# Another order for the first loads, the output stored in four parts, and another PSUM bank for two first up products

## The reference

```python
def first_block(x, ...):
    for i in range(2):
        xn = rms_norm(x, norm_mix[i])
        y = moba_attention(xn, w_qkv, w_o, cos, sin) if i == 0 else pool_mixer(xn, pool_w, pool_scale)
        x = x + y
        h = relu(rms_norm(x, norm_mlp[i]) @ w_up)       # 1024 -> 4096
        x = x + (h * h) @ w_down                        # 4096 -> 1024
    return rms_norm(x, norm_final)
```

## Time and profile before

| what | value |
|---|---|
| median of 3 runs | 1211.26 us (1208.13 to 1212.42) |
| the profiled execution's own time | 1212.48 us |
| its span, first to last instruction | 1210.7 us |
| TensorE busy | 1154.4 us, 95% of the span |
| VectorE busy | 676.7 us, 56% |
| ScalarE busy | 530.9 us, 44% |
| mean granted TensorE clock | 0.984 |
| start of the first product | 19.28 us |

### The profile page before, as it was taken

One profiled execution on the slowest core, in us unless ns is written; L12 is line 12 of the kernel. 1 busy time (PEld: TensorE's weight loads), 2 busy tenths in 40 slices (PEclk: granted clock), 3 DMA queues, 4 the chain that ended last, 5 costly groups with the idle time before them and its releaser, 6 DMA issues.

```text
span 1210.7 us, 17821 instructions
## 1 busy us (share of the span) xinstructions
PE 1154.4 (95%) x7132; PEld 1019.1 (84%) x7132; DVE 676.7 (56%) x933; ACT 530.9 (44%) x640; POOL 43.5 (4%) x69
## 2 busy tenths in 40 slices
PE   4999899999999999997898999999999999999997
PEld 4887799999889999977677999999888668999996
DVE  4745554455665544566545655555845556554554
ACT  5446344344443443444444443345433455344342
POOL 0000000000000000000000000002300410000000
PEclk9999999999999999998899999999999899999999
DMA  9751445645535556455313565556653222556550
GB/s 350 250 186 56 154 158 189 207 169 178 191 99 195 170 190 205 145 136 191 105 35 104 174 195 180 180 191 209 207 191 136 62 91 66 178 174 200 181 173 35
DMA packets 127450, 196.37 MB, mean 162 GB/s; under 512 B 7392, under 2 KB 97632, under 8 KB 127280
## 3 DMA queue, kind: packets, MB, share of 16 engines
q1 hardware_dynamic: 124256, 186.29, 46.6%
q0 software_dynamic: 3152, 9.51, 2.6%
HBM read 194.73 MB, written 1.05 MB: 162 GB/s over the span
## 4 chain that ended last, share of the span: by engine, by line
PE 84%; DVE 10%; ACT 3%; issue 1%; DMA 1%; DVEq 0%; SPq 0%; ACTq 0%
PE ps L1306 26%; PE ps L1307 25%; PE ps L1308 25%; DVE wlo L854 2%; DVE xs L942 1%; ACT whi L596 1%; PE ps L1443 1%; PE ps L1705 1%; PE ps L1428 1%; ACT junk L609 1%; DMA raw<-attn_w_qkv_in 1%; DVE act_lo L956 1%; PE ps L1664 1%; PE ps L1328 1%; DVE x L987 1%
## 5 line engine op out<-in xcount | busy, mean ns | idle before, releaser
L854 DVE TENSOR_TENSOR wlo<-raw,whi 128x2048 fp32r<-128x2048 f32 (+2 forms) x176 | 395.9, 2266 | 182.1 <-ACT whi L596 181.7
L1306 PE MATMUL ps<-act_hi,whi 128*128 128x256 f32 x1384 | 392.6, 284 | 7.7 <-DVE act_lo L956 4.7
L1307 PE MATMUL ps<-act_lo,whi 128*128 128x256 f32 x1384 | 391.7, 283 | 0.0
L1308 PE MATMUL ps<-act_hi,wlo 128*128 128x256 f32 x1384 | 391.6, 283 | 0.0
L596 ACT ACTIVATE whi<-raw 128x2048 fp32r<-128x2048 f32 (+2 forms) x176 | 328.8, 1888 | 118.6 <-PE ps L1308 104.0
L1306 PEld LDWEIGHTS ps<-act_hi,whi 128*128 128x128 f32 x1384 | 263.6, 190 | 12.5 <-issue 9.6
L1307 PEld LDWEIGHTS ps<-act_lo,whi 128*128 128x128 f32 x1384 | 263.6, 190 | 2.0
L1308 PEld LDWEIGHTS ps<-act_hi,wlo 128*128 128x128 f32 x1384 | 263.7, 191 | 0.0
L1308 PE MATMUL ps<-whi,hlo 128*128 128x512 f32 x400 | 156.8, 392 | 0.0
L1307 PE MATMUL ps<-wlo,hhi 128*128 128x512 f32 x400 | 156.8, 392 | 0.0
L1306 PE MATMUL ps<-whi,hhi 128*128 128x512 f32 x400 | 156.2, 390 | 0.0
(11 more groups left out here) (157 smaller groups left out, 906.6 us busy)
## 6 DMA issues: line engine op xcount, KB each, us to landing
raw<-mlp_w_up_in SPq DMA_DIRECT2D x32, 1024.0 KB, 6.3
raw<-mlp_w_down_in SPq DMA_DIRECT2D x32, 1024.0 KB, 4.9
raw<-ffn_w_gate_in SPq DMA_DIRECT2D x22, 1024.0 KB, 5.4
raw<-ffn_w_up_in SPq DMA_DIRECT2D x22, 1024.0 KB, 5.3
raw<-ffn_w_down_in SPq DMA_DIRECT2D x22, 1024.0 KB, 4.8
raw<-attn_w_qkv_in SPq DMA_DIRECT2D x12, 1024.0 KB, 8.6
raw<-w_kv_shared_in SPq DMA_DIRECT2D x8, 1024.0 KB, 6.7
raw<-attn_w_o_in SPq DMA_DIRECT2D x4, 1024.0 KB, 4.8
```

What stands on the lines that cost most here:

```text
L854: nc.vector.tensor_tensor(wlo[:, s, 0:width], raw[:, s, 0:width], whi[:, s, 0:width].bitcast(F32), ALU.subtract).then_inc(lo_ready, 1)
L1306: nc.tensor.matmul(dst, lhsT=left[0], rhs=right[0], start=start, stop=False, **kw)
L1307: nc.tensor.matmul(dst, lhsT=left[0], rhs=right[1], start=False, stop=False, **kw)
L1308: return nc.tensor.matmul(dst, lhsT=left[1], rhs=right[0], start=False, stop=stop, **kw)
```

## The change

SP's first transfers come in another order: `const` first, then x, then chunk 0 in two halves with a semaphore each, then chunk 1 and the next ones. The gain row of the first norm moves from SP to ScalarE's own DMA queue. The two loads of positions move from SP to POOL, where they come first, and POOL then waits until the high part of chunk 1 is made before it issues its rows. ScalarE and VectorE handle quarters 0 and 1 of the activation, then chunk 0 in two halves of 1024 columns, then quarters 2 and 3. TensorE makes chunk 0's products in another order, the first two groups of rows for both token tiles and then the other two, each after its half; ahead of the transposes it executes eight matmuls of the identity by itself into bank 7. In both MLP layers of the first block the first up product goes to bank 5 instead of 4, and the second up product no longer waits for `act_done`. At the end x is stored in four pieces of 256 KB, each as soon as it is written.

The diff:

```diff
--- before.py
+++ after.py
@@ -219,6 +219,9 @@
         w_used = sem("w_used")
         row_loaded = [sem(f"row_loaded{s}") for s in range(ROW_SLOTS)]
         first_row_loaded = sem("first_row_loaded")
+        first_half_loaded = sem("first_half_loaded")
+        first_half_hi = sem("first_half_hi")
+        first_half_lo = sem("first_half_lo")
         row_used = sem("row_used")
         x_loaded = sem("x_loaded")
         const_loaded = sem("const_loaded")
@@ -428,18 +431,13 @@
                     return
                 load(c, SLOT[c], source(kind, i), width, PREV[c] + 1 if PREV[c] >= 0 else None)
 
-            def first_row():
-                sp.dma_start(rows[:, 0, :], row_source["mix0"].partition_broadcast(P)
-                             .rearrange("q a n -> q (a n)")).then_inc(first_row_loaded, 16)
-
+            sp.dma_start(const[:, 0:C_CAUSAL], a["const"][:, 0:C_CAUSAL]).then_inc(const_loaded, 16)
             sp.dma_start(x[:, :, :], a["x"][0].rearrange("(t p) n -> p t n", p=P)).then_inc(x_loaded, 16)
-            first_row()
-            sp.dma_start(const[:, 0:C_CAUSAL], a["const"][:, 0:C_CAUSAL]).then_inc(const_loaded, 16)
-            load_one(0)
+            first = source("qkv", 0)
+            for h, landed in enumerate((first_half_loaded, w_loaded[SLOT[0]])):
+                sp.dma_start(raw[:, SLOT[0], h * D:(h + 1) * D].rearrange("p (k f) -> p k f", f=HALF),
+                             first[:, 2 * h:2 * h + 2]).then_inc(landed, 16)
             load_one(1)
-            for n, name in enumerate(("positions", "positions_2")):
-                sp.dma_start(pos_i[:, n, :], a[name].rearrange("a (t p) -> p (a t)", p=P),
-                             allow_slow_non_contiguous=True).then_inc(pos_loaded, 16)
             for c in range(2, AT["mlp0"]):
                 load_one(c)
                 if c == 5:
@@ -478,9 +476,11 @@
                     for c in range(AT["kvk"], AT["ffn1"]):
                         load_one(c)
             for t in range(TT):
-                sp.wait_ge(x_ready, 4 * 9 + 2 * (t + 1))
-                sp.dma_start(out[0, t * P:(t + 1) * P, :], x[:, t, :]).then_inc(out_stored, 16)
-            sp.wait_ge(out_stored, 16 * TT)
+                for h in range(2):
+                    sp.wait_ge(x_ready, 4 * 9 + 2 * t + h + 1)
+                    cols = slice(h * HALF, (h + 1) * HALF)
+                    sp.dma_start(out[0, t * P:(t + 1) * P, cols], x[:, t, cols]).then_inc(out_stored, 16)
+            sp.wait_ge(out_stored, 16 * 2 * TT)
 
 
         def scale_bias(pool, h):
@@ -537,6 +537,10 @@
                              bass.AP(table.tensor, h * REL, [[1, 64], [1, T]]))\
                   .then_inc(bias_loaded[h % 8], 16)
 
+            for n, name in enumerate(("positions", "positions_2")):
+                pool.dma_start(pos_i[:, n, :], a[name].rearrange("a (t p) -> p (a t)", p=P),
+                               allow_slow_non_contiguous=True).then_inc(pos_loaded, 16)
+            pool.wait_ge(hi_ready, 2)
             for name in ROWS[1:ROW["pre1"] + 1]:
                 load_row(name)
             pool.wait_ge(ffn[0].lo_done, NF)
@@ -624,9 +628,9 @@
                     sum_squares(name, t, x[:, t, :], D)
                 root(name, BOTH)
 
-            def copy_turned(name):
-
-                for p in range(4):
+            def copy_turned(name, parts=range(4)):
+
+                for p in parts:
                     act.wait_ge(turned, 4 * TURN[name] + p + 1)
                     nc.scalar.activation(act_quarter(act_hi, name, p), bank(4 + p).rearrange("p (k t) -> p k t", t=P),
                                          ACT.Copy).then_inc(act_hi_ready, 1)
@@ -665,7 +669,7 @@
                     act.wait_ge(w_used, n0 + 1 if first else i * 2 + n0)
                     if not first:
                         act.wait_ge(f.h_done, i)
-                    nc.scalar.activation(relu, bank(4), ACT.Relu).then_inc(f.act_done, 1)
+                    nc.scalar.activation(relu, bank(5 if first else 4), ACT.Relu).then_inc(f.act_done, 1)
 
                 def tail(i, first, last=False):
                     act.wait_ge(f.h_done, i + 1)
@@ -729,8 +733,15 @@
                 preload(ACT.Sqrt)
                 hi_before(n0 + 3 * (NF - 1) + 1)
 
-            hi_next()
-            copy_turned("mix0")
+            act.dma_start(rows[:, 0, :], row_source["mix0"].partition_broadcast(P)
+                          .rearrange("q a n -> q (a n)")).then_inc(first_row_loaded, 16)
+            copy_turned("mix0", (0, 1))
+            for h, landed in enumerate((first_half_loaded, w_loaded[SLOT[0]])):
+                act.wait_ge(landed, 16)
+                nc.scalar.activation(whi[:, SLOT[0], h * D:(h + 1) * D], raw[:, SLOT[0], h * D:(h + 1) * D],
+                                     ACT.Copy).then_inc(hi_ready if h else first_half_hi, 1)
+            cursor[0] = 1
+            copy_turned("mix0", (2, 3))
             hi_before(0)
             stats("mix0")
 
@@ -949,9 +960,9 @@
 
                 dve.sem_inc(row_used, 1)
 
-            def split_turned(name):
-
-                for p in range(4):
+            def split_turned(name, parts=range(4)):
+
+                for p in parts:
                     dve.wait_ge(act_hi_ready, 4 * ACTN[name] + p + 1)
                     nc.vector.tensor_tensor(act_quarter(act_lo, name, p), bank(4 + p).rearrange("p (k t) -> p k t", t=P),
                                             act_quarter(act_hi, name, p).bitcast(F32), ALU.subtract)\
@@ -1112,8 +1123,14 @@
             dve.sem_inc(x_ready, 4)
             for p in range(4):
                 gained("mix0", p)
-            lo_next()
-            split_turned("mix0")
+            split_turned("mix0", (0, 1))
+            for h, done in enumerate((first_half_lo, lo_ready)):
+                dve.wait_ge(hi_ready if h else first_half_hi, 1)
+                cols = slice(h * D, (h + 1) * D)
+                nc.vector.tensor_tensor(wlo[:, SLOT[0], cols], raw[:, SLOT[0], cols],
+                                        whi[:, SLOT[0], cols].bitcast(F32), ALU.subtract).then_inc(done, 1)
+            cursor[0] = 1
+            split_turned("mix0", (2, 3))
             lo_before(0)
             late_roots("mix0")
 
@@ -1332,6 +1349,8 @@
 
                 if name == "mix0":
                     pe.wait_ge(const_loaded, 16)
+                    for _ in range(8):
+                        nc.tensor.matmul(bank(7, 0, P), lhsT=ident, rhs=ident, start=True, stop=True)
                 for p in range(4):
                     h, t, _ = quarter(name, p)
                     if name in BUSY:
@@ -1456,11 +1475,11 @@
             def mlp_layer(f, norm):
                 n0 = f.first
 
-                def up(c, i, value, first=False):
+                def up(c, i, value, first=False, second=False):
                     wait_chunk(value)
-                    if not first:
+                    if not first and not second:
                         pe.wait_ge(f.act_done, i)
-                    tiles_out(slot(c), 4, norm if first else None).then_inc(w_used, 1)
+                    tiles_out(slot(c), 5 if first else 4, norm if first else None).then_inc(w_used, 1)
 
                 def down(c, i, value, first=False, last=False):
                     wait_chunk(value)
@@ -1470,7 +1489,7 @@
                              first, last, QUARTERS if last else None).then_inc(w_used, 1)
 
                 up(n0, 0, n0 + 1, True)
-                up(n0 + 1, 1, n0 + 2)
+                up(n0 + 1, 1, n0 + 2, second=True)
                 down(n0 + 2, 0, n0 + 3, first=True)
                 with pe.Fori(0, (NM - 2) // 2) as n:
                     for u in range(2):
@@ -1514,6 +1533,16 @@
             for n in range(6):
                 for kh in range(2):
                     c = 2 * n + kh
+                    if c == 0:
+                        wait_acts("mix0", 2)
+                        for h in range(2):
+                            pe.wait_ge(*((lo_ready, 1) if h else (first_half_lo, 1)))
+                            for t in range(TT):
+                                for k in range(2 * h, 2 * h + 2):
+                                    ins = product(bank(t), acts(k, t * P, (t + 1) * P),
+                                                  cols(slot(c), k * HALF, (k + 1) * HALF), start=k == 0, stop=False)
+                        ins.then_inc(w_used, 1)
+                        continue
                     wait_chunk(c + 1)
                     if n >= 2 and kh == 0:
                         pe.wait_ge(qkv_a, n - 1)
```

## The result

| | before | changed |
|---|---|---|
| median of 13 executions each | 1210.73 us | 1193.83 us |
| lowest, highest | 1208.13, 1213.86 | 1191.86, 1205.02 |
| ratio, 95% interval | | 0.9881 (0.9863 to 0.9900) |
| span of the profiled execution | 1210.7 us | 1193.3 us |
| its granted clock | 0.984 | 0.991 |

I had forecast 1201.8 and a range of 1198.5 to 1207.

A forecast was written before the change was run, and what follows sets the result against it. It took TensorE to bound the kernel (84% of the chain), idle for the first 19.28 us. Start 6.9, bank 5 2.0 and stores 0.6 made 9.5 us, so 1203.0 profiled and 1201.8 forecast, range 1198.5 to 1207.

The forecast's parts named there:

- The start: Start of the kernel, up to TensorE's first product: it begins at 12.4 instead of 19.28, saving 6.9 us.
- the landing of x and the row at 6.9 us: First loads: x, gain row and const, 1.66 MB, end at 6.6, plus 0.3 for the tail.
- rival 1: Start: the loads land later, the row at 8.69, POOL's rows perhaps ahead of chunk 3; 1204.5 us, chance 0.14.
- the halves' worth: Chunk 0 in halves: without them 1 us more in ScalarE and 1.1 in VectorE stand ahead of the first product.
- the eight extra matmuls: TensorE ahead of the transposes: they cost 1.8 us while it has nothing else to do.
- Nothing lost behind it: After the first product TensorE must not run dry; chunk 4 is tight with 2.6 us of slack left, no loss counted.
- rival 4: Start: positions through POOL land late and delay chunk 4; slower if after 37, 1216 if at 42; chance 0.04.
- Bank 5: First block's two MLP layers: the second up product follows the first at once, 1.0 us each, 2.0 us; bounds 1.6 and 2.1.
- The stores: End of the kernel: the halved last store lands 0.6 us sooner; bounds 0 and 1.3.
- The 0.3 that I had drawn from the Trainium skill: Last store: with a fixed cost of about 2.0 us per transfer, halving it would bring only 0.3 us.
- rivals 2 and 3: TensorE's clock at the start: low longer, 1205.0 or 1209.8 (0.08, 0.05); or high from the first product, 1200.2 (0.07).
- rival 3: Start: the clock is high from the first product, 1.6 us more, 1200.2; chance 0.07.

The follow-up runs named there:

- steady: Changed kernel plus busy matmuls in the second block's pauses: nine in the long one, three ahead of each attention's first score; ratio 0.9849, 1190.7 to 1192.8 us.
- scores_only: Kernel before plus three busy matmuls ahead of the first score of each of the second block's two attentions; ratio 0.9922, 1202.3 to 1203.8 us.
- the added matmuls: Busy matmuls where TensorE has no pause: two or three in the kernel before (0.9981, 1.0016), two in the changed kernel (1192.2 to 1204.9 us).
- the fills: Busy matmuls in the second block's pauses, put into the changed kernel (ratio 0.9849) and into the kernel before (0.9929).
- bank_only: Kernel before with only the first up product in bank 5 and the second one's wait dropped; ratio 0.9922, ten of 12 executions 1199.3 to 1200.4 us.
- x_first: Changed kernel with x issued ahead of const on SP; ratio 0.9903, first product at 16.05 us.

## Why the prediction missed

**The start (6.9 us; 3.85 in the trace, 5.0 in `steady`).** The step that failed is the landing of x and the row at 6.9 us: the transfers' end at 6.6, by "418 GB/s with x and one row in flight", and the "0.3 for the tail" behind it. x landed at 10.0. The DMA view of the kernel before from 3 to 5.5 us, by queue (packets, MB, share), shows what nearly all of the 418 GB/s between 4 and 6 us were:

```profile
DMA packets 266, 1.02 MB, mean 410 GB/s; under 512 B 16, under 2 KB 16, under 8 KB 266
## 3 DMA queue, kind: packets, MB, share of 16 engines
q1 hardware_dynamic: 266, 1.02, 103.0%
```

That is SP's queue alone, so x and only behind it the first part of the gain row, not two queues side by side; POOL's rows (q0), issued at 1.24, moved nothing before 5.6. I had taken an issue for a transfer. In the changed kernel, from 1.5 to 4.5 us:

```profile
DMA packets 277, 0.61 MB, mean 203 GB/s; under 512 B 22, under 2 KB 150, under 8 KB 277
...
q10 hardware_dynamic: 130, 0.50, 52.0%
q1 hardware_dynamic: 147, 0.11, 21.6%
```

There ScalarE's queue (q10) moves the row beside SP's (q1) `const`, 128 packets of 704 bytes, and x waits behind `const`. From 1 to 4 us all queues moved 168 GB/s where I had used 199, and from 4 to 6 us 336 where I had used 418; with the 303 up to 7.5 us the 1.66 MB were through near 7.6 (an estimate from these three rates), 1.0 us late. The larger part came after it: x's last packets landed 2.4 us later, at 10.0, for a tail of 0.3. From 7 to 8.5 us the positions' packets moved and the rate was down to 208 GB/s; with the positions issued later it was 404 and x landed at 8.3. How much of the tail is theirs stays open, since one kernel with them early had x at 8.5. My rival 1 named late loads, and 8.69 for the row as its worst; it was x, at 10.0.

The steps from there on came out: 5.2 us to the first product (5.5 forecast), the halves' worth 1.7 (2.1), and eight distances of 0.43 us in the profiled execution, as I had kept. One price was wrong without harm: the eight extra matmuls took 3.8 us, not 1.8, and ended before the late x.

**Nothing lost behind it: right.** TensorE has no wait from 16 us to the moba attention. VectorE's bank copy for chunk 4 ended at 36.40 and TensorE came to it at 39.0, a slack of 2.6 as forecast. The positions through POOL (rival 4) landed 6.3 and 8.1 us after their issue, long before their conversion at 28.1; what I had not priced is that they share the DMA with x.

**Bank 5 (2.0 us): right.** The lead is 3.6 us behind chunk 3, 4.6 in layer 0 and 5.6 in layer 1, so 1.0 us for each. In the changed kernel the starts run on at 0.12 while relu works beside them:

```profile
140.60 0.28 PE L1324 MATMUL ps<-act_lo,whi 128*128 128x256 f32 x1
140.72 0.28 PE L1325 MATMUL ps<-act_hi,wlo 128*128 128x256 f32 x1
140.84 0.28 PE L1323 MATMUL ps<-act_hi,whi 128*128 128x256 f32 x1
```

**The stores (0.6 us): right by the trace.** A store lands 2.1 us after its issue, for 2.6: 0.5 us. The 0.3 that I had drawn from the Trainium skill (DMA: Bandwidth & Descriptors) is further off, but that was my use of it: the fixed 2.0 us stand in its section Anatomy of one DMA, fitted to transfers that GpSimd issues, and go with 436 GB/s for the bytes. Taken whole, the fit gives 0.6 us for the halved store, near the measured 0.5, and 3.2 us for the one of 512 KB, where the trace has 2.6; SP issues these.

**The clock: the case that wasn't on my list.** I looked at the clock only where the change touched TensorE, at the start (rivals 2 and 3). The page of before showed three fallen slices in its row of 40, all in the second block, and I passed them over because the diff doesn't touch them. The clock was worth 11.2 us of the 17.4 between the two profiles. `scores_only` shows that most of it can be had without the change, and the added matmuls that moving the same work in time is enough to bring or avoid it. The change's own steps gave 6.2 us in the profile and 7.5 with the pauses filled, both under the sum of 9.5. That the sum lies near the 9.7 us of the ratios with the fills is luck: the start gave 1.9 us less at the first product, and the clock, high from the first product as in my rival 3 and longer in the second block, gave 3.8 back. What stays open: which shift gives which odds. I forecast none of these, and no run tells the moment of the clock's changes ahead.

## What to carry to other kernels

Read the clock column for the whole program before summing gains at one end of it: where it falls in stretches of small work, moving the work ahead can change whether it falls again, and an edit far away can win or lose several times its own worth (`bank_only`: 2.0 us of its own, 9.5 by the ratio). Fill the short pauses in those stretches with busy matmuls, here 3 x 0.44 us ahead of each attention's first score, and compare edits on that ground. And take the bandwidth of a stretch with the queues that moved bytes in it: an issued DMA is not yet a moving one, and small packets of another queue may, by the rates here, hold up the end of a large transfer.

## What the runs showed of the hardware that I had not expected

- Three busy matmuls in each of two pauses of 1.5 and 0.8 us, ahead of small matmuls, kept the low stretches of 13.6 and 10.2 us away in the profiled execution of `scores_only`, and all its five executions at or under 1203.8; nine in a pause of 5.6 us did not, and 6.8 us of the low stretch in and behind that pause stayed.
- The same kernel comes out in groups 8 to 12 us apart, by its granted clock (0.994 against 0.981 for `bank_only`), on one core with nothing else in the program changed.
- POOL's DMAs issued at 1.24 us moved their first bytes between 5.6 and 5.8 us at the start of this program (in the changed kernel issued at 1.25, first bytes after 6.2); ScalarE's, issued at 0.73, between 1.8 and 2.0.
- With 512 runs of 4 bytes on POOL's queue between 6 and 8.5 us, the DMA moved 162 to 301 GB/s from 7 to 8.5 us in seven kernels, and 404 in the one with the same order of loads that issued them later.
- A 128 x 128 float32 matmul of the identity by itself took 0.47 us (3.78 us for eight, each two instructions), twice a transpose of the same size at its slower pace (3.67 us for 16, 0.23 each); where the transposes came fast, 16 took 2.0 us (`x_first`).
